# Rows of two experts gathered already turned, in place of a gather and a turn for each

## What is computed

```
logits = xt @ w_router + b_router            # 288 tokens of 1024, 32 experts
top_v, top_e = top_k(logits, 4); gate = softmax(top_v)
for each expert e, over the tokens that picked it (rows xb):
    h  = xb @ w_gu[e] + b_gu[e]              # 1024 -> 2 x 1024
    gt = min(h[:, :1024], 7); up = clip(h[:, 1024:], -7, 7)
    ye = ((up + 1) * gt * sigmoid(1.702 * gt)) @ w_dn[e] + b_dn[e]
    y[token] += gate * ye
out = layernorm(ALPHA * h_in + y) * ln2_g + ln2_b
```

## Time and profile before

| | |
|---|---|
| timed runs | 1400.37, 1401.36 and 1401.50 us, median 1401.36 |
| profiled execution, first to last instruction (span) | 1399.1 us |
| profiled execution, its own total | not listed; the timed runs are 1.3 to 2.4 us above the span |
| mean granted TensorE clock | 0.995 of full speed |
| PE, DVE, ACT, POOL busy | 98%, 31%, 21%, 7% |
| HBM read | 471.8 MB, 343 GB/s over the span |
| loop over experts | 464 to 1382 us of the span |

### The profile page before, as it was taken

How to read it: one execution, slowest core, us unless ns; L and a number is a source line. 1 busy time by engine, 2 the same in 40 slices (tenths; PEclk the granted TensorE clock), 3 DMA queues, 4 the chain that set the end, 5 groups by cost and what they waited for, 6 DMA issues and landing times.

```text
span 1399.1 us, 20516 instructions
## 1 busy us (share of the span) xinstructions
PE 1371.1 (98%) x7816; PEld 653.1 (47%) x7816; DVE 434.3 (31%) x956; ACT 294.5 (21%) x504; POOL 93.2 (7%) x122
## 2 busy tenths in 40 slices
PE   9999999999999999999999999999999999999996
PEld 6667999867775333333333333333333333333332
DVE  0345764863336311221113111221122111221114
ACT  1125531352312111111112111111111111111101
POOL 0031400203000000000000000000000000000000
PEclk9999999999999999999999999999999999999998
DMA  8831340738796899999999999999999999999994
GB/s 295 293 101 57 110 167 16 210 117 270 214 356 266 360 374 425 428 428 427 429 428 429 429 428 430 428 428 428 429 429 430 427 428 429 429 429 428 426 429 158
DMA packets 79327, 477.05 MB, mean 341 GB/s; under 512 B 9686, under 2 KB 38054, under 8 KB 54374
## 3 DMA queue, kind: packets, MB, share of 16 engines
q1 hardware_dynamic: 75028, 465.12, 82.2%
q0 software_dynamic: 2288, 9.51, 1.9%
q10 hardware_dynamic: 1954, 1.63, 0.4%
HBM read 471.81 MB, written 8.59 MB: 343 GB/s over the span
## 4 chain that ended last, share of the span: by engine, by line
PE 87%; DMA 10%; DVE 1%; ACT 1%; issue 0%; SPq 0%
PE bank L1401 27%; PE bank L1444 14%; DMA big<-in_w_gu 10%; PE bank L1049 5%; PE bank L1337 4%; PE bank L1316 4%; PE bank L811 3%; PE bank L795 2%; PE bank L1218 2%; PE bank L866 2%; PE bank L868 2%; PE bank L874 2%; PE bank L1307 2%; PE bank L1236 2%; PE bank L1430 1%; PE bank L1327 1%
## 5 line engine op out<-in xcount | busy, mean ns | idle before, releaser
L1401 PE MATMUL bank<-big,gates 128*64 128x512 f32 x1536 | 338.6, 594 | 5.6 <-DMA big<-in_w_gu 5.4
L1401 PEld LDWEIGHTS bank<-big,gates 128*64 128x64 f32 x1536 | 107.0, 137 | 218.1 <-issue 204.2
L1444 PE MATMUL bank<-big,gates 128*64 128x512 f32 x768 | 171.4, 595 | 0.0
L2578 DVE TENSOR_SCALAR gates<-bank 128x512 f32<-128x512 f32 x32 | 22.1, 691 | 433.7 <-PE bank L1415 433.7
L1759 ACT ACTIVATE gates<-gates 128x512 f32<-128x512 f32 x32 | 20.1, 630 | 454.7 <-DVE gates L2578 454.7
L1444 PEld LDWEIGHTS bank<-big,gates 128*64 128x64 f32 x768 | 53.0, 137 | 114.1 <-issue 114.1
L1846 POOL TENSOR_TENSOR gates<-gates,nsaT 128x192 f32<-128x192 f32 x64 | 31.4, 511 | 977.1 <-PE bank L1349 859.8
L2602 DVE TENSOR_TENSOR work<-work,bank 128x512 f32<-128x512 f32 x124 | 79.4, 682 | 41.2 <-PE bank L1337 41.2
L2598 DVE TENSOR_TENSOR work<-work,bank 128x256 f32<-128x256 f32 x31 | 13.0, 421 | 195.9 <-PE bank L1340 195.9
L1774 ACT ACTIVATE gates<-bank 128x512 f32<-128x512 f32 x31 | 18.5, 597 | 250.3 <-PE bank L1340 250.3
L1337 PE MATMUL bank<-gates 64*128 64x512 f32 x248 | 70.0, 641 | 0.0
(11 more groups left out here) (427 smaller groups left out, 1621.4 us busy)
## 6 DMA issues: line engine op xcount, KB each, us to landing
big<-in_w_gu SPq DMA_DIRECT2D x96, 2048.0 KB, 23.0
big<-in_w_dn SPq DMA_DIRECT2D x48, 2048.0 KB, 26.2
front_rows<-in_w_gu SPq DMA_DIRECT2D x16, 2048.0 KB, 23.6
front_cols<-in_w_gu SPq DMA_DIRECT2D x15, 2048.0 KB, 21.8
front_cols<-in_w_dn SPq DMA_DIRECT2D x8, 2048.0 KB, 26.4
front_rows<-in_w_dn SPq DMA_DIRECT2D x8, 2048.0 KB, 28.8
big<-in_w_in SPq DMA_DIRECT2D x5, 2048.0 KB, 8.5
big<-in_cache_cmp_kv SPq DMA_DIRECT2D x64, 128.0 KB, 2.6
```

The source lines that it names most:

```text
L1401: last = pe.matmul(psum[2 + n][half * CAP:(half + 1) * CAP, :], xe[:, k % 4, (k // 4) * CAP:(k // 4 + 1) * CAP], weights_gu(slot, k % 2, c ...
L1444: last = pe.matmul(psum[5][half * CAP:(half + 1) * CAP, :], act_T[:, k % 4, (k // 4) * CAP:(k // 4 + 1) * CAP], ring_dn[slot][:, k % 4, ha ...
```

## The change

Picks are made for two experts at once, and the gather swaps its operands: the tokens' rows are the stationary operand and the picks of two experts (128 columns) are the moving one, so that the result stands already turned. `turn_rows`, `xg` and ACT's copy of it go. The turned rows of a pair are four tiles `xe[pair parity][half]`; each expert gathers one half of the next pair's rows, so both buffers alternate. `h_perm` holds the tokens' rows in an order in which a 128-wide slice is one chunk; `scale_half` writes it with strided operands, and `start_rows` reads it back in order. The sums move to the old `h_rows`. In `w_gu`, a piece no longer holds two adjacent rows of a 256-row block for each partition but two of the four rows of a 512-row block. POOL weighs two experts at a time, ACT's loop holds four experts and DVE's two. The last two experts gather nothing. Before the loop both halves of the first pair are gathered, into banks 1 and 0, and the turn and the two `keep_busy` calls are gone.

```diff
-        xg = part(xT, 0, [512])
+        h_perm, y_sum = y_rows, h_rows
-        xe = part(gates, 0, [4, P])
+        xe = [[part(gates, 0, [4, P]), part(xT, 0, [4, P])],
+              [part(work, 2 * D + D // 4, [4, P]), part(gates, 3968, [4, P])]]
-        pick_rows = part(gates, 3968, [3, CAP])
-        pg = part(gates, 4160, [3, 2, CAP])
+        pick_rows = part(small, 0, [3, 2, CAP])
+        pg = part(work, 6 * D, [2, 3, 2, CAP])
...
                 if j < 4:
-                    src, dst = ins["w_gu"][0, bass.ds(e, 1), 2 * j * P:(2 * j + 2) * P, :], ring_gu[slot]
+                    src, dst = ins["w_gu"][0, bass.ds(e, 1), j // 2 * 4 * P:(j // 2 + 1) * 4 * P, :], ring_gu[slot]
+                    rows = slice(2 * (j % 2), 2 * (j % 2) + 2)
...
-                sp.dma_start(dst, src.rearrange("o (p a) n -> (o p) a n", p=P)).then_inc(piece_loaded[slot], 16)
+                sp.dma_start(dst, src.rearrange("o (p a) n -> (o p) a n", p=P)[:, rows, :]).then_inc(piece_loaded[slot], 16)
...
-                for half in range(2):
-                    pe.matmul(psum[0][half * CAP:(half + 1) * CAP, :], pick_rows[0:NS, 2, :],
-                              h_rows[0:NS, 2, half * 512:(half + 1) * 512], start=True, stop=False, skip_group_check=True)
+            def gather_sample(pair, half, bank=1):
+                pe.wait_ge(pick_ready, pair + 1)
+                if pair is 0:
+                    pe.wait_ge(h_ready, half + 1)
+                for c in range(4):
+                    d0 = (4 * half + c) * P
+                    for m in range(2):
+                        own = slice(m * DH, (m + 1) * DH)
+                        pe.matmul(psum[bank][own, c * P:(c + 1) * P], h_perm[0:NS, 2, d0 + m * DH:d0 + (m + 1) * DH],
+                                  pick_rows[0:NS, 2, :, :], start=(c == 0), stop=False, skip_group_check=True)
...
+            def gather(pair, half, bank=1):
                 for t in range(2):
+                    if pair is 0:
+                        pe.wait_ge(h_ready, 3 + 2 * t + half)
+                    for c in range(4):
+                        d0 = (4 * half + c) * P
+                        last = pe.matmul(psum[bank][:, c * P:(c + 1) * P], h_perm[:, t, d0:d0 + P], pick_rows[:, t, :, :],
+                                         start=False, stop=(t == 1), skip_group_check=True)
                 last.then_inc(gathered, 1)
-            def turn_rows(n):
-                pe.wait_ge(xg_copied, n + 1)
-                if n is not 0:
-                    pe.wait_ge(xe_copied, n)
-                for c in range(4):
-                    last = pe.transpose(psum[1][:, c * P:(c + 1) * P], xg[:, c // 2 * 256 + c % 2:c // 2 * 256 + 256:2], ident)
-                last.then_inc(xe_turned, 1)
...
+                    if of == 0 and k % 4 == 0:
+                        pe.wait_ge(xe_copied, pair * 2 + 1 + k // 4)
...
                 pe.wait_ge(sel_ready, i + 1)
                 pe.wait_ge(ye_copied, i + 1)
-                if not final:
-                    gather_sample(i + 1)
+                if more_rows:
+                    pe.wait_ge(xe_copied, i + 2)
+                    gather_sample(pair + 1, of)
...
                     combine(i, 0)
-                    gather(i + 1)
+                    if more_rows:
+                        gather(pair + 1, of)
...
-                    turn_rows(i + 1)
                     combine(i, 1)
...
-            gather_sample(0)
-            gather(0)
-            keep_busy(1)
-            turn_rows(0)
-            keep_busy(1)
+            for half in range(2):
+                gather_sample(0, half, 1 - half)
+                gather(0, half, 1 - half)
...
+            def take_rows(pair_at, half, n, bank=1):
+                act.wait_ge(gathered, n)
+                act.activation(xe[pair_at][half], psum[bank][:, :].rearrange("p (c n) -> p c n", c=4), ACT.Copy).then_inc(xe_copied, 1)
...
-                if not final:
-                    take_turned(i + 1)
...
+            def weigh_pair(e2, pair):
+                pool.wait_ge(pick_ready, pair + 1)
+                pool.wait_ge(pg_turned, pair * 2 + 1)
+                for of in range(2):
+                    for half in range(2):
+                        last = pool.tensor_tensor(pg[:, of, :, half, :], pick_rows[:, :, of, :],
+                                                  gate[:, :, bass.ds(e2 * 2 + of, 1)].broadcast_to([P, 3, CAP]), ALU.mult)
                 last.then_inc(pg_ready, 1)
...
-                dve.scalar_tensor_tensor(out=x, in0=x, scalar=ln_rstd[0:m, at:at + 1], in1=ln1[0:m, 1, cols], op0=ALU.mult, op1=ALU.add).then_inc(h_ready, 1)
+                dve.scalar_tensor_tensor(out=h_perm[0:m, t, cols].rearrange("p (a q) -> p a q", a=4),
+                                         in0=x.rearrange("p (q a) -> p a q", a=4), scalar=ln_rstd[0:m, at:at + 1],
+                                         in1=ln1[0:m, 1, cols].rearrange("p (q a) -> p a q", a=4),
+                                         op0=ALU.mult, op1=ALU.add).then_inc(h_ready, 1)
...
+            def pick_slots(pair):
+                if pair is not 0:
+                    dve.wait_ge(gathered, pair * 2)
+                    dve.wait_ge(pg_ready, pair)
+                dve.tensor_tensor(pick_rows, C("slot_of").unsqueeze(1).unsqueeze(1).broadcast_to([P, 3, 2, CAP]),
+                                  (place if pair is 0 else place_all)[:, :, bass.ds(pair * 2, 2)].unsqueeze(3).broadcast_to([P, 3, 2, CAP]),
+                                  ALU.is_equal).then_inc(pick_ready, 1)
```

## The result

| | before | after |
|---|---|---|
| median of 7 timed runs each | 1400.67 us | 1404.70 us |
| spread | 1399.76 to 1401.50 | 1402.88 to 1405.45 |
| span of the profiled execution | 1399.1 us | 1402.2 us |
| that execution's own time | not listed | 1403.99 us |

A forecast was written before the change was run, and what follows sets the result against it. Transfers were taken to set the end, with 0.30 us of PE room per expert; a period of 28.41 - 0.10 + 0.49 = 28.80 and a start 0.94 us later make it PE-bound: 1401.4 + 3.3 = 1404.7 us, range 1401.3 to 1412.5.

The forecast's parts named there:

- What bounds the kernel: Expert loop: transfers set the end; PE's period of 28.41 us has 0.30 us of room, up to 28.71.
- (a): Steady expert: removing the turn's 0.67 us of PE gains only 0.10 us, as the combine waits for DVE's additions.
- (b): Steady expert: gather of the two full tiles, 16 records where there were 8, costs zero.
- (c): Steady expert: sample tile's gather ahead of the biases delays them by 0.49 us in each expert that gathers.
- (d): Before the loop: gathering both halves of the first pair, 2.90 us, makes the start 0.94 us later.
- (e): SP's queue: w_gu pieces read as 16 KB of every 32 KB, no change in speed.
- (f): Last pair: expert 30 gathers nothing, so its period is 28.31 us.
- The sum: Last expert's biases begin at 1371.3 against 1368.0 us: +3.3 us, PE-bound throughout, 1404.7 us.
- hidden after all: Rival for the sample gather: biases start beside it, period 28.31, transfers set the end, 1402.1 us; chance 0.28.
- strictly one behind the other: Rival for the sample gather: matmuls start strictly in order, period 29.12, +12.9 us, 1414.3 us; chance 0.25.
- a little under 428 GB/s: Sign of being right: transfers in the changed kernel's profile move slightly below 428 GB/s.
- the dry stretch: Transfers run dry at 514 to 518 us; the next piece's issue at 516.75 moves 1.7 us later.

The follow-up runs named there:

- e10: Kernel before with the combine of tile 1 moved between the two halves of the down product: 1400.85 us, ratio 1.0002.
- e5: Kernel before with one idle matmul of 256 columns added behind the down product of every expert but the last: 1410.85 us, ratio 1.0070.
- e4: Kernel before with the turn taken out and nothing in its place (output not the reference's): 1398.94 us, ratio 0.9988.
- e7: Changed kernel with the sample gather's loops swapped, four matmuls of one array tile first, then four of the other: 1419.82 us, ratio 1.0134.
- e3: Changed kernel with the sample tile's gather issued twice in each expert of the loop: 1431.51 us, ratio 1.0226.
- e1: Changed kernel with the sample gather issued behind the six bias matmuls instead of ahead of them: 1401.88 us, ratio 1.0009.
- e11: Changed kernel with DVE's small copy behind tile 0's additions and four unread matmuls where expert 30 has no gather: 1402.46 us, ratio 1.0013.
- e12: As e11, with the sample gather also behind the biases, against the changed kernel: 1401.16 us, ratio 1.0004.
- e8: Kernel before with only the change's new layout of the w_gu pieces (output not the reference's): 1401.13 us, ratio 1.0000.
- item 10: Granted clocks behind expert 30 compared across runs, plus two kernels with filler matmuls there, e11 and e12: 1402.46 and 1401.16 us.
- e2: Changed kernel with DVE's small copy select_row moved behind the additions of tile 0: 1403.01 us, ratio 1.0017.
- e9: e1's kernel with the combine of tile 1 moved between the two halves of the down product: 1403.35 us, ratio 1.0018.
- e0: Changed kernel timed again without any edit, beside the edits of it: 1403.93 us, ratio 1.0027.

## Why the prediction came out right

*What bounds the kernel: right.* Periods of 28.69 (e10) and 29.05 (e5) on the kernel before cost 0.0 and 10.0 us; the room of 28.71 predicts 0 and 10.5.

*(a) The turn gives 0.10: right.* 0.09 in e4, and the combine starts 0.05 us after DVE's additions in after, 0.15 us after them in before.

*(b) The gather of full tiles, zero: right in effect.* It takes 1.90 us (481.95 to 483.85), under the cover of DVE.

*(c) The sample gather, +0.49: right, by its row.* The L967 rows said "at about the fifth of its eight"; measured 0.49, and e7 and e3 fit the same queue at 0.99 and 1.37. The Trainium skill (TensorE: Matmul & The Clock Gate, Part 3) states strict FIFO for MATMULs, in their starts and in their ends. This case's traces don't agree for the starts: six records of the gather start behind the first bias, which stands behind them in the program (479.96 against 479.86 in after; three in e7). By the strict reading the time would have been 1414.3; 1404.7 was measured.

*(d) The start, +0.94: mis-sized by 0.2.* Measured +1.13 from the pick's start. The pick's 0.2 came as predicted. The halves take 3.00 us each and not 2.90: 1.02 for the sample tile (1.01 was taken) and 1.98 for the full tiles, for which 1.89 was taken from a set that is followed by its own shape. The strided scaling did get slower, 1.14 us for 0.75, but nothing of it counts: DVE's next operation starts 0.79 us behind PE's last product ahead of it in both kernels (457.31 to 458.10, 457.54 to 458.33). Single profiles place the start when they are read from a common point, the last long `keep_busy` call at full clock. From there the loop is 10.87 us away in after (454.61 to 465.48), e1, e11 and e12, and 9.73 in e10, whose start is that of the kernel before: +1.14. Before's own execution had a granted clock of 0.52 from 453.6 to 457.1 us, which made this stretch 10.52 us, and its earlier stages ran 1.0 us ahead of after's; the two about cancel.

*(e) The pieces, no change: right*, by e8.

*(f) Last pair: right in its period*, 28.28 for 28.31. That its missing gather leaves PE idle for 1.8 us, and that the clock can fall behind it (item 10), was not seen. In after's profile it did not fall; in some of its timed runs it probably did (item 10).

The sum: the last biases at 1371.14, predicted 1371.3; the median 1404.70, predicted 1404.7. That both agree so well is luck. In the profile the loop began 0.42 us later than predicted (465.48 for 465.06), and thirty periods of 28.78 for 28.80 took it back. In the median the base was 0.7 too high (1401.4 from three runs, 1400.67 from seven) and the rise as much too small (3.3 for 4.03). The 2.3 us said to lie around the span were too many as well: the profiled execution of after took 1403.99 with a span of 1402.2. The second measurement gave 1403.93. A rise of 3.3 to 4.0 us for a predicted 3.3, by a mechanism that the experiments bear out, is not luck. The rival "hidden after all" would have been 1402.1; e1 builds just that case (block of 1.06, period 28.29), and came to 1401.88. The rival "strictly one behind the other" is refuted by the timeline. One sign of being right failed: transfers "a little under 428 GB/s" were forecast, and they moved at 428; a period of 28.78 us is still under the 29.4 that a full queue needs for an expert. A side sum was off: the dry stretch ended 2.1 us later than before in the profile (518.84 against 516.75), predicted 1.7; it had no effect, as PE set the end.

Left open: how many records a tile's queue holds exactly. Three waiting fit all offsets (0.50, 0.99, 1.37) and the counts of six, three and six records behind the first bias, but only sets of 32-row, 128-column records were tried.

## What to carry to other kernels

Where two resources are nearly level, work out the room between them first: here 0.30 us for each expert, below which work on PE is free and above which every 0.1 us costs 3 us. Then look at who waits next: removing 0.67 us of turning gave 0.10, since DVE's additions were due then anyway, and moving the combine away uncovered ACT's copy. Independent matmuls on other row groups overlap only as far as PE gets to issue them: put the few long ones first and the many small ones, which queue on one tile, behind them. And an idle time of PE in one late expert can cost more than its own length, in some executions, by the clock behind it.

## What the runs showed of the hardware

- Sixteen short records ahead of six biases cost 0.49 us, behind them 0.02 (block of 1.06 for 1.04); fed one tile after the other, 0.98.
- DVE's 128x512 `scalar_tensor_tensor` took 1.14 us with strided operands where its plain form takes 0.75 (L2483 and L2478 of after), and ACT's 128x1024 activation reading `h_perm` in strides 2.09 us, for 1.05 in order in before (L1725).
- A bias started ahead of six matmul records that stood before it in PE's program, since these belonged to two tiles that were still busy (after); of one busy tile it was three (e7).
- Behind the 1.8 us of idle PE in expert 30 the granted clock fell to 0.50 in the profiled executions of e2, e7 and e9 and stayed at 1.00 in those of after, e0, e1 and e3. In e7 the fall made 5.84 us of work 8.90.
- Breaking a run of equal matmuls with four of another shape cost 0.15 us beside their own 1.06 us (e9: 3.58 and 3.59 us for the halves, 7.02 for the whole).
- Pieces read as 16 KB of every 32 KB move at 428 GB/s, as solid ones do.
